# Expert weights of two neighbouring blocks in one 4 MB transfer, with the SBUF arena in another order

## The reference, cut to what matters

```python
N_EXPERTS, TOP_K, D_MODEL, D_EXPERT = 32, 4, 1024, 1024

def expert_block(toks, wts, e):          # for every expert e and its tokens
    xb = hf[toks]
    gu = xb @ w_gate_up[e] + b_gate_up[e]              # (., 1024) @ (1024, 2048)
    gate, up = gu[:, :D_EXPERT], gu[:, D_EXPERT:]
    gate = jnp.minimum(gate, 7.0)
    up = jnp.clip(up, -7.0, 7.0)
    glu = gate * jax.nn.sigmoid(1.702 * gate)
    y = ((up + 1.0) * glu) @ w_down[e] + b_down[e]     # (., 1024) @ (1024, 1024)
    return y * wts[:, None]
```

## Time and profile before

| what | value |
|---|---|
| median of 3 executions | 1204.24 us (1202.94 to 1204.4) |
| the profiled execution: its own device time | 1205.32 us |
| its span, first to last instruction | 1203.5 us |
| TensorE busy with matmuls | 1127.1 us, 94% |
| VectorE, ScalarE busy | 427.3 us, 152.3 us |
| granted TensorE clock, mean | 0.990 |
| read from HBM | 462.93 MB, 386 GB/s over the span |
| chain that ended last | TensorE 73%, DMA 20%, VectorE 3%, ScalarE 3% |

### The profile page before, as it was taken

How to read it: one execution, slowest core, us unless ns; L and a number is a source line. 1 busy time by engine, 2 the same in 40 slices (tenths; PEclk the granted TensorE clock), 3 DMA queues, 4 the chain that set the end, 5 groups by cost and what they waited for, 6 DMA issues and landing times.

```text
span 1203.5 us, 13253 instructions
## 1 busy us (share of the span) xinstructions
PE 1127.1 (94%) x5366; PEld 523.5 (43%) x5366; DVE 427.3 (36%) x946; ACT 152.3 (13%) x332; POOL 0.4 (0%) x6
## 2 busy tenths in 40 slices
PE   5999999999999999999999999998989899989896
PEld 1787688855333333333333333333333333332332
DVE  5478166423723324131314233141313131313133
ACT  2111133301011010101010110101010101010102
POOL 0000000000000000000000000000000000000000
PEclk9999999998999999999999999999999999999999
DMA  9998923397999999999999999999999999999994
GB/s 361 402 380 356 412 76 140 140 379 273 386 426 427 429 427 426 428 429 426 428 429 427 428 427 427 430 426 426 428 429 428 427 427 428 427 427 427 429 425 173
DMA packets 37587, 464.75 MB, mean 386 GB/s; under 512 B 4224, under 2 KB 4800, under 8 KB 9376
## 3 DMA queue, kind: packets, MB, share of 16 engines
q1 hardware_dynamic: 35792, 461.11, 91.7%
q10 hardware_dynamic: 1744, 2.88, 0.7%
HBM read 462.93 MB, written 1.05 MB: 386 GB/s over the span
## 4 chain that ended last, share of the span: by engine, by line
PE 73%; DMA 20%; DVE 3%; ACT 3%; issue 1%; ACTq 0%; SPq 0%; DVEq 0%
PE ps L949 27%; DMA arena<-in_w_gate_up 18%; PE ps L975 14%; PE ps L672 7%; PE ps L936 5%; PE ps L982 3%; PE ps L806 2%; PE ps L829 2%; PE ps L761 2%; PE ps L893 2%; ACT arena L1284 1%; PE ps L662 1%; ACT arena L1277 1%; DMA arena<-in_w_ada 1%; DVE arena L1473 1%
## 5 line engine op out<-in xcount | busy, mean ns | idle before, releaser
L949 PE MATMUL ps<-arena 128*64 128x512 f32 x2048 | 454.7, 599 | 13.1 <-DMA arena<-in_w_gate_up 13.0
L949 PEld LDWEIGHTS ps<-arena 128*64 128x64 f32 x2048 | 143.9, 138 | 319.8 <-issue 291.8
L975 PE MATMUL ps<-arena 128*64 128x512 f32 x1024 | 226.8, 595 | 9.6 <-ACT arena L1277 9.6
L1716 DVE TENSOR_SCALAR arena<-ps 128x512 f32<-128x512 f32 x32 | 22.1, 692 | 430.6 <-PE ps L949 430.6
L975 PEld LDWEIGHTS ps<-arena 128*64 128x64 f32 x1024 | 70.6, 137 | 144.6 <-issue 130.9
L1273 ACT ACTIVATE arena<-arena 128x512 f32<-128x512 f32 x32 | 20.2, 630 | 742.0 <-DVE arena L1716 742.0
L672 PE MATMUL ps<-arena 128*128 128x256 f32 x448 | 97.6, 379 | 0.0
L672 PEld LDWEIGHTS ps<-arena 128*128 128x128 f32 x448 | 85.0, 190 | 13.6 <-issue 2.3
L1758 DVE TENSOR_TENSOR arena<-ps,arena 64x512 f32<-64x512 f32 x64 | 44.1, 689 | 122.9 <-PE ps L975 122.2
L936 PEld LDWEIGHTS ps<-arena 128*128 128x128 f32 x512 | 58.4, 192 | 12.2 <-issue 12.2
L936 PE MATMUL ps<-arena 128*128 128x128 f32 x512 | 61.4, 278 | 0.0
(11 more groups left out here) (244 smaller groups left out, 609.8 us busy)
## 6 DMA issues: line engine op xcount, KB each, us to landing
arena<-in_w_gate_up SPq DMA_DIRECT2D x127, 2048.0 KB, 38.2
arena<-in_w_down SPq DMA_DIRECT2D x61, 2048.0 KB, 36.6
arena<-in_w_ada SPq DMA_DIRECT2D x11, 2048.0 KB, 17.0
arena<-in_w_in SPq DMA_DIRECT2D x9, 2048.0 KB, 17.4
arena<-in_w_down SPq DMA_DIRECT2D x6, 1024.0 KB, 42.2
arena<-in_w_ada SPq DMA_DIRECT2D x2, 1024.0 KB, 24.7
arena<-in_w_in SPq DMA_DIRECT2D x2, 1024.0 KB, 28.5
arena<-in_w_hy_out SPq DMA_DIRECT2D x1, 2048.0 KB, 15.9
```

The costliest lines, as they stand in the source:

```text
L949: last = mm(ps[64 * h:64 * h + 64, 4 + b, :], hTp[:, k, s * 64:(s + 1) * 64], w[:, o:o + 512], start=False, stop=(k == KD - 1))
L975: last = mm(ps[64 * h:64 * h + 64, out_bank, :], lhs, rows[:, qq * D + h * 512:qq * D + (h + 1) * 512], start=(q == 0), stop=(q == 7))
```

## The change: joined transfers and the order of the arena

The arena's regions are put in another order and `ring` is cut into six regions, so that slots 0, 1, 2, 3, 4, 5 lie one behind another, and so do 8, 9, 10. The host lays w_gate_up out as two rows of 32 KB per partition and expert in place of four of 16 KB, and w_down as one of 32 KB in place of two of 16 KB. In pairs 1 to 14, where block n has an even place in its pair and slot n mod 11 is 0, 1, 2, 3, 4, 8 or 9, blocks n and n+1 come in one transfer of 4 MB (128 rows of 32 KB), and one semaphore, that of the first slot, stands for both. The transfer is issued when both slots are free. All other blocks, and those of pairs 0 and 15, come as before, with rows of 16 KB (or 8 KB, in the halves) that now lie 32 KB apart in HBM. 54 such joined transfers replace 108 of 168 single ones in pairs 1 to 14. No instruction of TensorE, VectorE or ScalarE is added or removed.

```diff
-                ("ring", 24576), ("dft", 1024), ("inv", 1024), ("qm", 2048), ("ur", 12 * 258), ("uc", 3072),
-                ("kf", 2560), ("x", 2048), ("adr", 1536), ("on", 512), ("xn", 2048), ("ht", 2048),
-                ("kt", 1024), ("ve", 1024), ("sc", 1024), ("at", 512), ("ab", 512),
+                ("ring2", 4096), ("dft", 1024), ("inv", 1024), ("qm", 2048), ("ring3", 4096),
+                ("kt", 1024), ("ve", 1024), ("sc", 1024), ("at", 512), ("ab", 512), ("ring4", 4096), ("ring5", 4096),
+                ("ring0", 4096), ("ring1", 4096), ("x", 2048), ("adr", 1536), ("on", 512),
+                ("ur", 12 * 258), ("uc", 3072), ("kf", 2560), ("xn", 2048), ("ht", 2048),
...
-        ring = [at("ring", 4096 * s, 4096) for s in range(6)]
+        ring = [at(f"ring{s}") for s in range(6)]
...
-        uses_before = [sum(n % NS == k for n in range(PAIR * FIXED)) for k in range(NS)]
+        NEXT_TO = {0: ("ring2", 0), 1: ("dft", 0), 2: ("ring3", 0), 3: ("kt", 0), 4: ("ring4", 0), 8: ("ring0", 0), 9: ("ring1", 0)}
+
+        def joined(n):
+
+            return n >= NS + 1 and n % PAIR % 2 == 0 and n % NS in NEXT_TO
+
+        landings = [0] * NS
+        landing = []
+        for n in range(PAIR * FIXED):
+            if n and joined(n - 1):
+                landing.append(landing[-1])
+            else:
+                landings[n % NS] += 2 if n == HALVED else 1
+                landing.append((n % NS, landings[n % NS]))
...
-                return slots[n % NS], s_slot[n % NS], 16 * (n // NS + 1) + 16 * (n % NS == HALVED)
+                k, count = landing[n]
+                return slots[n % NS], s_slot[k], 16 * count
...
+                cols = slice(4096 * (j % 2), 4096 * (j % 2) + 4096)
+                src = w_gu[expert, j // 2][:, cols] if isinstance(expert, int) else w_gu[bass.ds(expert, 1), j // 2, :, cols]\
...
+            def both(p, i, src):
+
+                name, off = NEXT_TO[(PAIR * p + i) % NS]
+                free(p, i + 1)
+                sp.dma_start(span(name, off, 8192), src).then_inc(place(p, i)[1], 16)
+
             def pair_of(p, e_a, e_b):
 
-                for j in range(NJ):
-                    free(p, A0 + j)
-                    gate_up(place(p, A0 + j), e_a, j)
-                for c in range(NC):
-                    free(p, DA + c)
-                    down(place(p, DA + c), e_a, c)
...
+                for first, expert in ((A0, e_a), (B0, e_b)):
+                    for j in range(0, NJ, 2):
+                        if joined(PAIR * p + first + j):
+                            both(p, first + j, w_gu[expert, j // 2])
+                        else:
+                            for i in (j, j + 1):
+                                free(p, first + i)
+                                gate_up(place(p, first + i), expert, i)
+                    down_at = DA if first == A0 else DB
+                    if joined(PAIR * p + down_at):
+                        both(p, down_at, w_dn[expert, 0])
+                    else:
+                        for c in range(NC):
+                            free(p, down_at + c)
+                            down(place(p, down_at + c), expert, c)
...
         if name == "w_gate_up":
-            v = v[0].reshape(E, 4, 2, P, 2 * FE).transpose(0, 1, 3, 2, 4).reshape(E, 4, P, 4 * FE)
+            v = v[0].reshape(E, 2, 4, P, 2 * FE).transpose(0, 1, 3, 2, 4).reshape(E, 2, P, 8 * FE)
         elif name == "w_down":
-            v = v[0].reshape(E, 2, 4, P, D).transpose(0, 1, 3, 2, 4).reshape(E, 2, P, 4 * D)
+            v = v[0].reshape(E, 1, 8, P, D).transpose(0, 1, 3, 2, 4).reshape(E, 1, P, 8 * D)
```

More of the change, by code:

```diff
@@ L395, in place @@
                 n = PAIR * p + i
-                return slots[n % NS], s_slot[n % NS], 16 * (n // NS + 1) + 16 * (n % NS == HALVED)
+                k, count = landing[n]
+                return slots[n % NS], s_slot[k], 16 * count
             k = fixed_slot[i]
-            return slots[k], s_slot[k], p * 16 + 16 * (uses_before[k] + 1 - FIXED + (k == HALVED))
+            return slots[k], s_slot[k], p * 16 + 16 * (landings[k] + 1 - FIXED)
         def piece(c):
@@ L453, in gate_up @@
                 dst, landed, _ = place_
-                src = w_gu[expert, j] if isinstance(expert, int) else w_gu[bass.ds(expert, 1), j]\
+                cols = slice(4096 * (j % 2), 4096 * (j % 2) + 4096)
+                src = w_gu[expert, j // 2][:, cols] if isinstance(expert, int) else w_gu[bass.ds(expert, 1), j // 2, :, cols]\
                     .rearrange("o p n -> p (o n)")
@@ L459, in down @@
                 dst, landed, _ = place_
-                src = w_dn[expert, c] if isinstance(expert, int) else w_dn[bass.ds(expert, 1), c]\
+                cols = slice(4096 * c, 4096 * c + 4096)
+                src = w_dn[expert, 0][:, cols] if isinstance(expert, int) else w_dn[bass.ds(expert, 1), 0, :, cols]\
                     .rearrange("o p n -> p (o n)")
@@ L484, in _ @@
             sp.wait_ge(S["mix_ps"], 3)
-            sp.dma_start(dst[:, 0:2048], w_gu[1, 3][:, 0:2048]).then_inc(landed, 16)
+            sp.dma_start(dst[:, 0:2048], w_gu[1, 1][:, 4096:6144]).then_inc(landed, 16)
             wait_used(blocks[-1])
-            sp.dma_start(dst[:, 2048:4096], w_gu[1, 3][:, 2048:4096]).then_inc(landed, 16)
+            sp.dma_start(dst[:, 2048:4096], w_gu[1, 1][:, 6144:8192]).then_inc(landed, 16)
             sp.wait_ge(S["x1_rdy"], 5)
@@ L524, in looped_pair @@
                         free(p, L_DB + c // 2)
-                    sp.dma_start(piece(c), w_dn[bass.ds(e_b, 1), c // 2, :, 2048 * (c % 2):2048 * (c % 2 + 1)]
+                    sp.dma_start(piece(c), w_dn[bass.ds(e_b, 1), 0, :, 2048 * c:2048 * (c + 1)]
                                  .rearrange("o p n -> p (o n)")).then_inc(s_last[c], 16)
@@ L532, in _ @@
             sp.wait_ge(S["half_used"], 1)
-            sp.dma_start(first_again[:, 0:2048], w_dn[1, 1][:, 0:2048]).then_inc(S["half_in"], 16)
+            sp.dma_start(first_again[:, 0:2048], w_dn[1, 0][:, 4096:6144]).then_inc(S["half_in"], 16)
             free(0, DB + 1)
-            sp.dma_start(first_again[:, 2048:4096], w_dn[1, 1][:, 2048:4096]).then_inc(landed, 16)
+            sp.dma_start(first_again[:, 2048:4096], w_dn[1, 0][:, 6144:8192]).then_inc(landed, 16)
             for p in range(1, FIXED):
```

## The result

The changed kernel took 1209.2 us (median of 5 executions, 1207.06 to 1210.22) against 1203.33 us of the kernel before (5 executions, 1202.94 to 1204.4, beside it on the chip). The ratio is 1.0043 with a 95% interval of 1.0032 to 1.0054, so it is slower by 3.9 to 6.5 us.

What follows compares the result with a forecast made beforehand. The prediction took the DMA as the bound up to block 177's landing, with TensorE's work behind it. Its terms, 4.8 - 4.1 + 3.5 = +4.2 us, added to the median of 1204.24 gave 1208.4 us, range 1203.0 to 1212.5.

Steps and rivals of the forecast that it cites:

- What bounds the kernel: From 320 us the DMA never pauses, early idling returns at the end; block 177's landing at 1117.61 us ends the bound.
- Fewer packets: Joined transfers between blocks 20 and 177: 9 packets fewer per engine at 9.0 ns, 81 ns each, 4.1 us saved.
- The late start: Start of pair 1: joined blocks 14 and 15 wait for both slots and land one block's time later, +4.8 us.
- It just holds: Blocks 20 and 21: engines busy until about 343.4 us, their first packet due at 342.5, so no further idle time.
- Two blocks at once: Blocks 176 and 177: TensorE cannot begin 176 before both land, so it has one block more to do, +3.47 us.
- Behind block 177: After block 177: no wait for blocks 178 and 179, and the rest behind it 82.3 us as before.
- the rival that had a chance of 0.10 and a time of 1206.7: Rival: pauses and work come at other moments, so the clock's loss of 1.7 us at 1138 us may not recur.
- Priced at nothing: Arena order, front part, SyncE's fewer issues, landing counts, and 16 KB rows lying 32 KB apart: no cost.
- A 32 KB row as two packets: Rival: in joined transfers only the small packets are saved, +7.9 us, 1212.1 us; chance 0.10.
- Better streaming: Rival: long rows stream better than the packet price says, 0.2 us saved per joined transfer, 1202.3 us; chance 0.14.
- A fixed cost per transfer: Rival: 54 fewer transfers free the DMA so far that no late pair waits, some 1184 us; chance 0.04.
- The fall of the clock in the longer pauses: Rival: longer waits ahead of blocks 174 and 176 lower TensorE's clock; if low after the last, 1210.1 us; chance 0.20.

Runs made afterwards that it cites:

- the kernel with the bare waits: No joined transfers; where the changed kernel joins, both single transfers wait for both slots, arena and layout as changed: 1207.3 us, ratio 1.0033 to the kernel before.
- the second trace of the changed kernel: The changed kernel, unaltered, measured and profiled again in a later series: 1208.43 us, ratio 1.0040 to the kernel before.
- the version with both losses undone: The changed kernel, joined only from block 30 on and with blocks 174 to 177 single: 1200.63 us, ratio 0.9969; repeated, 1200.62 us, ratio 0.9973.
- the kernel with one wait of TensorE: The kernel before, no transfer touched, TensorE also waiting for block 177 before it begins block 176: 1208.6 us, ratio 1.0039.

## Why the prediction was right, step by step

Forecast: 1208.4 us, +4.2 on the median. Measured: a ratio of 1.0043, which is 1.0032 to 1.0054 or +3.9 to +6.5 us. The three terms forecast are those that the runs show, and each was measured by itself. What lies behind block 177 didn't stay as forecast in the traces, and a part of the agreement is luck; the fifth point says how much.

- **What bounds the kernel.** The last transfer of the chain is block 177 in both traces, and what lies behind it carries the end. That a microsecond of idle DMA near 310 us is still there at 1117 us is shown by the kernel with the bare waits (+4.0 us in the time, 4.2 at the landing of block 177).
- **Fewer packets.** Forecast 0.081 us per joined transfer, 4.1 in all. The landings give 0.07 to 0.08, the traces of before and after 3.4 us in all (4.8 - 1.37), the second trace of the changed kernel 3.9, the version with both losses undone 3.3 to 3.7 with 45 joined transfers ahead of block 177. The price of a packet drawn from 4 KB and 16 KB rows held for 32 KB rows to about a sixth.
- **The late start.** Forecast +4.8, seen as 13.2 against 8.4 us to landing, and 4.0 (2.6 to 5.4) in the time by itself. "It just holds" of blocks 20 and 21 was right: there was no gap at them in the changed kernel, and with 14 and 15 single there is one. By the prediction's rows they would then land 3.5 us later than before, and they landed 2.4 us later; from issue to landing they took 12.1 us, 2.4 more than their 9.7 us of transfer, where the prediction took 3.5 from block 15.
- **Two blocks at once.** Forecast +3.47, seen as 3.42 in the chain and confirmed from both sides: taken out of the changed kernel it leaves +1.1 us, put into the kernel before it gives 3.3 to 6.1. That the same costs nothing in earlier pairs holds to within 2 us.
- **Behind block 177.** Forecast: the same 82.3 us of TensorE's work as before. Both traces of the changed kernel have 80.5, since the fall of the clock at 1138 us is missing: the rival that had a chance of 0.10 and a time of 1206.7 is what the traces show. In the 13 profiled executions of this document the four blocks there take 15.58 us in five, the kernel before among them, and in all of these TensorE takes block 177 alone. They take 13.88 us in all six in which TensorE takes 176 and 177 together, and in two others. So the grain of two may bring this gain with it; the kernel with one wait of TensorE shows it too, in its single trace, but no run tests that by itself. By the traces alone the loss is 1.4 + 3.4 - 1.7 = 3.1 us in the first and 0.9 + 3.4 - 1.7 = 2.6 in the second, and the ratios say 3.9 to 6.5 and 3.1 to 6.5. Both profiled executions were the fastest of their five. Some 2 us of the measured loss stand in no trace, and without them the forecast would have been too high: that its middle was met so closely is in part luck.
- **Priced at nothing.** Arena and layout: ratio 0.9996.
- **The rivals.** A 32 KB row as two packets: out, by the packet count. Better streaming: out, 9.71 us per joined transfer where it needed 9.6. A fixed cost per transfer: out; 4 MB and short rows, with 54 transfers fewer, gained no rate at all. The Trainium skill's 2.0 us of fixed cost per transfer, which the prediction set beside this rival (DMA: Bandwidth & Descriptors, "Anatomy of one DMA"), is a fit for transfers that GpSimd issues, and SyncE issues these. In a full queue the traces here show nothing of such a cost: 2 MB land every 4.89 us, and 4 MB of short rows every 9.79. The fall of the clock in the longer pauses: it exists (8.46 us for 32 matmuls in the kernel joined from block 20 on, 8.82 in the one with TensorE's wait), but behind the last pause both profiled executions of the changed kernel were free of it, and both were free of the old loss at 1138 us too. How these two balance over many executions wasn't settled. A fall in the last pause of the slower executions would account for most of the 2 us that stand in no trace; that is not shown.

The kernel joined from block 20 on, where the last pause was 2.62 us and the clock did fall:

```profile
1106.03 7.09 PE L975 MATMUL ps<-arena 128*64 128x512 f32 x32 [2.47 <-DMA arena<-in_w_gate_up]
1115.74 8.46 PE L975 MATMUL ps<-arena 128*64 128x512 f32 x32 [2.62 <-DMA arena<-in_w_gate_up]
```

```profile
1110.00:1115.00 5.00, 3.11 (x16) 0.80 (x12) 0.00 (x0) 0.00 (x0) 0.00 (x0) 1.00 1.03 441
1115.00:1120.00 5.00, 4.26 (x14) 1.43 (x16) 0.00 (x0) 0.00 (x0) 0.00 (x0) 0.66 0.95 406
```

## What to carry to other kernels

Longer rows save packets wherever the DMA is the bound; a larger transfer of the same short rows gained nothing that shows. Its grain cost at two places here: where the queue is short, since the transfer must wait for all of its room before any of it can start, and at the last landing that the end waits for, since the consumer then has all of it still to do. Join in the middle and leave the two ends fine; here that turned 5 us lost into some 3.5 us won, from the same idea. When a kernel passes from a compute bound to a DMA bound, time the DMA idles in the early, compute-bound part is not free: look at the time to landing, which shows how short the queue is.

## What was not expected of the hardware

The clock fell after quite different pauses and stayed up after others of the same length: low after 2.39 and 2.62 us in two kernels, full after 2.63 and 2.83 us in the changed one. Even in one execution of the changed kernel it stayed up after the longer pause and fell after the shorter:

```profile
851.95 7.09 PE L975 MATMUL ps<-arena 128*64 128x512 f32 x32 [3.37 <-DMA arena<-in_w_gate_up]
911.49 8.70 PE L975 MATMUL ps<-arena 128*64 128x512 f32 x32 [2.62 <-DMA arena<-in_w_gate_up]
```

The length of the pause just before does not decide it alone. The falls shown so far took 1.4 to 1.7 us each from a run of 32 matmuls of 512 columns; two in the versions with both losses undone took 2.6 and 2.9 us (9.65 us after a pause of 3.69, 10.03 after one of 3.35). By the chains, a fall told in the time only where no landing was waited for afterwards. In the kernel joined from block 30 on, the fall ahead of blocks 174 and 175 only shortened the next wait:

```profile
1102.56 8.66 PE L975 MATMUL ps<-arena 128*64 128x512 f32 x32 [1.86 <-DMA arena<-in_w_gate_up]
1112.28 7.09 PE L975 MATMUL ps<-arena 128*64 128x512 f32 x32 [1.06 <-DMA arena<-in_w_gate_up]
```
